# A hybrid decoder block on one core: logits in four column groups, new orders in the routing loop and at its end

## The chip, the cores and the metric

The kernel runs on one core of one Trainium2 chip. The metric is the device time of one execution in microseconds (us). Before the change the median of three runs was 2406.98 us (2404.17 to 2409.48).

## The reference, cut to what matters

1024 tokens of width 1024 go through a mixer (gated linear attention and a short convolution, merged by gates), then through a mixture of 32 experts of which each token uses four. The change touches only what lies between the two.

```python
x = x + jnp.matmul(mixed, w_out[l])
h = rms_norm(x, g_ffn[l])
logits = jnp.matmul(xt, w_router) + b_router      # (1024, 32), float32
top_logit, top_idx = lax.top_k(logits, TOP_K)     # 4 of 32
gates = jax.nn.softmax(top_logit, axis=-1)
...                                               # tokens sorted by expert
gu = lax.ragged_dot(xs, w_gate_up, group_sizes) + b_gate_up[e_sorted]
act = (lin + 1.0) * (gate * jax.nn.sigmoid(SWIGLU_ALPHA * gate))
out = lax.ragged_dot(act, w_down, group_sizes) + b_down[e_sorted]
y = jnp.einsum("tkd,tk->td", out_pairs, gates.astype(out.dtype))
```

## The kernel before

The program is a row of blocks, one after the other; each has a hand-written instruction stream for every engine, ordered by semaphores, and a block ends for all engines together, when the last of them is through. Five engines matter: PE (matmul), ACT, DVE (vector), POOL, which also issues the indirect DMAs, and SP, which issues the plain ones.

**The block `output_and_route`** multiplies the mixer's result with `w_out`, adds it to x, and routes. TT = 8 tiles of P = 128 tokens. The last panel of `w_out` (256 columns) is done tile by tile, in a loop in which the routing of the tiles in front is woven in. In iteration i PE does: two of the eight row blocks of the product of tile i; `turn(i-1)`, eight transposes of x2; three more row blocks; `rank(i-2)`; `logit(i-1)`, eight float32 matmuls whose left operand is `wr`, 128 x 32, and whose right one is a 128 x 128 block of the turned tile; the last three row blocks; `turn_back(i-1)`, a transpose of the 32 x 128 logits. ACT does per tile: `square` (sum of squares), `move` (the turned tile out of PSUM), `exps` of the tile in front (the exponentials of the four top logits), `root` (square root) and `move_low` (the logits out of PSUM). Exp and square root lie in different activation tables. DVE does per tile, in this order: `seats(i-2)` (the seat of each token in its expert's list, then the gates, written with them in `slots` and `place`, then the signal `slotted`), `select(i-2)` (two comparisons into `sel`, from which the rows of expert 0 are listed), `invert(i-1)`, `add(END-1, i)`, which signals `taken`, `choose(i-1)` (top 4) and `norm(i-1)` (the normed rows `ht`, stored to `h_rows` by SP). POOL writes, for each tile with `slotted`, TOP_K = 4 indirect scatters of `slots` into the table `slot_rows` (L1716); just ahead of the second scatter of tile 7 it waits for `first_listed` and for all stores of `h_rows` and issues the gather `xg` of the rows of expert 0 (L1713). SP stores x2 and ht of each tile and, between the x2 and the ht of the last tile, loads the weight panels m = 2, 3 of expert 0 (2 x 1 MB).

After the loop: `list_first` on DVE (L1841, L1843) gives the rows of expert 0; DVE splits a weight panel (L1906); then a chain of small operations (L1911 to L1939) with three matmuls plans the loop over the experts; DVE copies the plan (L1942 to L1947). PE transposes the gathered rows (L2049), ACT and DVE split them into `x_hi` and `x_lo` (L1774, L1951), and the block ends.

**The block `experts`** follows. SP loads m = 4 to 7 at once, and m = 8 to 11 when PE has done two panels. POOL issues the gather `xs_g` (L2331), waits for both gathers, reads the list of the next rows out of `slot_rows` (L2261, L2264) and then gathers the rows of the next 128-token unit (L2271). PE does panels 0 and 1, waits for `xs_g`, transposes it (L2686), does panels 2, 3, the small spill products (L2748), which run in four column groups of 32, then enters a loop over the units; in its first turn it transposes the next rows (L2679), and waits for them there. ACT and DVE split each panel (L2396, L2521); the first one on DVE in this block is L2656.

## Time and profile before

| | us |
|---|---|
| median of three runs | 2406.98 |
| lowest, highest | 2404.17, 2409.48 |
| the profiled execution | 2403.14 |
| its span, first to last instruction | 2401.6 |
| PE busy in the span | 2341.9 (98%) |
| DVE, ACT, POOL busy | 1629.0, 1273.5, 374.7 |

Times in rows are us from the span's start. A busy time of PE is not PE at its peak: matmuls overlap in the records. A timeline row gives start, duration, engine, line, operation, what it writes and reads, and in brackets the idle time ahead of it and what ended that. "POOLq" and "SPq" are the queues' own instructions. PEclk is the granted TensorE clock as a share of 2.4 GHz. The routing block runs its last tile loop from 999 to 1047, the experts start at 1072.

### The profile page before, as it was taken

The numbers are of one execution on the slowest core, as the hardware profiler recorded it, in microseconds if no ns is written. First come the engines' busy times: TensorE is split into PE (matmuls) and PEld (weight loads), VectorE is DVE, ScalarE is ACT, GpSimd is POOL, SyncE is SP. The second block draws the span as 40 slices with busy tenths as digits, with TensorE's granted clock in tenths as the row PEclk, the third lists the DMA queues.
The fourth block names the chain that finished last, engine by engine and source line by source line (L and its number), as shares of the span: only waits on it lengthen the run. The fifth ranks groups of instructions, "written<-read, shape, count | busy, mean of one in ns | idle before, by whom it ended". The sixth has DMA issues, their size and how long they took to land.

```text
span 2401.6 us, 40275 instructions
## 1 busy us (share of the span) xinstructions
PE 2341.9 (98%) x13219; PEld 1875.2 (78%) x13316; DVE 1629.0 (68%) x1669; ACT 1273.5 (53%) x1358; POOL 374.7 (16%) x412
## 2 busy tenths in 40 slices
PE   9999999999999999979999999999999999999996
PEld 7887778888888887957788777777777887777775
DVE  5213557766765353377798786878777987778877
ACT  6314663223233121365677666767656775667766
POOL 0000000000000002452211212112212122112110
PEclk9999999999999999989999999999999999999998
DMA  5233325454335235358999889989889997989998
GB/s 131 41 48 53 101 63 126 67 73 72 71 71 210 98 130 159 137 184 309 348 385 380 305 297 315 377 310 377 297 281 343 385 380 266 348 308 377 339 346 309
DMA packets 264860, 553.35 MB, mean 230 GB/s; under 512 B 29497, under 2 KB 76345, under 8 KB 263666
## 3 DMA queue, kind: packets, MB, share of 16 engines
q1 hardware_dynamic: 241490, 497.32, 61.9%
q0 software_dynamic: 23296, 55.03, 8.1%
q8 instruction: 48, 0.79, 0.1%
q14 instruction: 26, 0.21, 0.0%
HBM read 501.28 MB, written 51.02 MB: 230 GB/s over the span
## 4 chain that ended last, share of the span: by engine, by line
PE 53%; DMA 1%; issue 1%; DVE 0%; POOLq 0%; ACT 0%; DVEq 0%; ACTq 0%
PE m_y L2709 5%; PE m_y L2711 5%; PE m_y L2710 5%; PE m_gate L2711 5%; PE m_gate L2709 5%; PE m_lin L2711 5%; PE m_lin L2709 5%; PE m_gate L2710 5%; PE m_lin L2710 5%; PE m_spill L2748 4%; PE m_spill L2760 2%; PE m_turn L2693 1%; PE m_lin L2717 1%; PE m_gate L2679 1%; PE m_lin L2679 1%
## 5 line engine op out<-in xcount | busy, mean ns | idle before, releaser
L2521 DVE TENSOR_TENSOR m_w_lo<-raw,m_w_hi 128x2048 fp32r<-128x2048 f32 x382 | 868.7, 2288 | 245.2 <-ACT m_w_hi L2396 243.1
L2396 ACT CAST m_w_hi<-raw 128x2048 fp32r<-128x2048 f32 x382 | 730.9, 1914 | 353.3 <-PE m_lin L2711 243.9
L126 PE MATMUL c_bank<-h_hi_r,ring_hi 128*128 128x512 f32 x656 | 259.0, 395 | 1.9 <-DVE qk_r L1436 0.9
L2709 PE MATMUL m_gate<-m_w_hi,x_hi 128*128 128x512 f32 x508 | 215.8, 425 | 0.0
L2709 PE MATMUL m_y<-m_w_hi,m_a_hi 128*128 128x512 f32 x512 | 210.3, 411 | 1.8 <-DVE m_a_lo L2569 1.8
L2711 PE MATMUL m_y<-m_w_hi,m_a_lo 128*128 128x512 f32 x512 | 200.0, 391 | 0.0
L2710 PE MATMUL m_y<-m_w_lo,m_a_hi 128*128 128x512 f32 x512 | 199.7, 390 | 0.0
L2711 PE MATMUL m_gate<-m_w_hi,x_lo 128*128 128x512 f32 x508 | 198.8, 391 | 0.0
L2709 PE MATMUL m_lin<-m_w_hi,x_hi 128*128 128x512 f32 x508 | 198.4, 391 | 0.0
L2711 PE MATMUL m_lin<-m_w_hi,x_lo 128*128 128x512 f32 x508 | 198.3, 390 | 0.0
L2710 PE MATMUL m_gate<-m_w_lo,x_hi 128*128 128x512 f32 x508 | 198.2, 390 | 0.0
L2710 PE MATMUL m_lin<-m_w_lo,x_hi 128*128 128x512 f32 x508 | 197.8, 389 | 0.0
L128 PE MATMUL c_bank<-h_lo_r,ring_hi 128*128 128x512 f32 x480 | 187.3, 390 | 0.0
L905 ACT CAST ring_hi<-ring_raw 128x512 fp32r<-128x512 f32 x126 | 78.4, 624 | 189.7 <-PE c_bank L129 141.0
L126 PEld LDWEIGHTS c_bank<-h_hi_r,ring_hi 128*128 128x128 f32 x656 | 123.1, 188 | 34.7 <-issue 7.1
L2292 POOL DMA_INDIRECT y_rows<-m_y_out,m_slot_out x31 | 66.0, 2130 | 502.2 <-ACT m_y_out L2431 273.0
L129 PE MATMUL c_bank<-h_hi_r,ring_raw_r 128*128 128x512 f32 x368 | 143.6, 390 | 0.0
L172 ACT CAST ring_hi<-ring_raw 128x2048 fp32r<-128x2048 f32 x25 | 47.8, 1910 | 157.8 <-DMA ring_raw<-in_w_out 59.1
L176 DVE TENSOR_TENSOR ring_raw_r<-ring_raw,ring_hi 128x2048 fp32r<-128x2048 f32 x25 | 57.7, 2308 | 106.6 <-ACT ring_hi L172 106.5
L1055 DVE TENSOR_TENSOR ring_hi<-ring_raw,ring_hi 128x512 fp32r<-128x512 f32 x126 | 86.8, 689 | 59.6 <-ACT ring_hi L905 59.5
L2709 PEld LDWEIGHTS m_y<-m_w_hi,m_a_hi 128*128 128x128 f32 x512 | 96.6, 189 | 29.4 <-issue 6.9
L2271 POOL DMA_INDIRECT xg<-h_rows,slot_in x32 | 67.4, 2105 | 323.8 <-PE m_lin L2686 196.7
(425 smaller groups left out, 4606.0 us busy)
## 6 DMA issues: line engine op xcount, KB each, us to landing
raw<-in_w_gate_up SPq DMA_DIRECT2D x512, 512.0 KB, 11.3
raw<-in_w_down SPq DMA_DIRECT2D x256, 512.0 KB, 12.4
ring_raw<-in_w_in SPq DMA_DIRECT2D x31, 1024.0 KB, 9.6
gates<-work POOLq DMA_DIRECT2D x32, 256.0 KB, 4.4
work<-gates SPq DMA_DIRECT2D x8, 1024.0 KB, 7.2
v<-in_x SPq DMA_DIRECT2D x8, 512.0 KB, 5.3
r_rows<-work POOLq DMA_DIRECT2D x16, 256.0 KB, 3.0
o_rows<-v SPq DMA_DIRECT2D x8, 512.0 KB, 11.1
```

The lines of the kernel that those rows point to most:

```text
L126: pe.matmul(out, left_hi(k), right_hi(k), start=first and k == kts[0], stop=False, skip_group_check=True)
L128: pe.matmul(out, left_hi(k), right_lo(k), start=False, stop=False, skip_group_check=True)
L129: mm = pe.matmul(out, left_lo(k), right_hi(k), start=False, stop=last and k == kts[-1], skip_group_check=True)
L905: act.copy(ring.form(m)[0], ring.block(n, *((0, 0), (0, 0), (1, 0), (1, 0), (0, 1), (1, 1), (0, 1))[f])) \
L1055: dve.tensor_tensor(lo, (a11, a11, a21, a21, a12, a22, a12)[f], f32(hi), ALU.subtract) \
L2271: pool.indirect_dma_start(out=xg[:, :], out_offset=None, in_=h_rows[:, :], in_offset=bass.IndirectOffsetOnAxis(ap=slot_in[:, 0, 0:1], axis ...
L2396: act.copy(w_hi[:, p % WS].rearrange("p k b n -> p (k b n)"), raw[:, raw_slot(m)].rearrange("p k b n -> p (k b n)")).then_inc(signals.whi, 1)
L2521: dve.tensor_tensor(w_lo[:, p % WS].rearrange("p k b n -> p (k b n)"), raw[:, raw_slot(m)].rearrange("p k b n -> p (k b n)"), f32(w_hi[:, ...
L2709: pe.matmul(out, left_hi[:, kt], right_hi, start=False, stop=False, skip_group_check=True)
L2710: pe.matmul(out, left_hi[:, kt], right_lo, start=False, stop=False, skip_group_check=True)
L2711: mm = pe.matmul(out, left_lo[:, kt], right_hi, start=False, stop=kt == KT - 1, skip_group_check=True)
L2748: mm = pe.matmul(into(g), xs[:, 2 * (m % 4) + k], raw[:, raw_slot(m), k, :, P * g:P * g + P], start=False, stop=m % 4 == 3 and k == 1, ski ...
```

## The change

It does six things.

1. `logit`: the eight matmuls go to four column groups, k % 4, into the partitions 32g to 32g + 31 of `p_low`. `move_low` copies 128 partitions instead of 32, and `turn_back` is a float32 matmul with a constant `fold` (128 x 32, four identities), which adds the four parts.
2. ACT: `exps` are done for two tiles at a time, in odd iterations; in even ones `move_low` comes ahead of `root`.
3. DVE: `seats` no longer waits for the exponentials. The gates and the signal `slotted` are in a new `weigh`, called for tile i - 3 at the end of iteration i, and for tiles 5, 6, 7 after the planning chain (behind L1939). The two comparisons of `select` are one (`mark`) against a constant `seat_no`; at the end `norm(7)` comes ahead of `choose(7)`.
4. POOL: the tiles 0 to 4 are scattered (20 scatters), then it waits for `first_listed` and the stores and issues the gather `xg`; then tiles 5 and 6 (8 scatters), then the gather `xs_g`, all in the routing block. The four scatters of tile 7 are the first indirect DMAs of POOL in the block `experts`; ahead of the next list POOL waits until the last twelve scatters have landed (`end_sent`).
5. SP: the panels m = 2, 3 are loaded behind the last store of `h_rows`; m = 4 to 7 are loaded in the routing block too, when `xg` has landed.
6. The last block of DVE: `x_lo` is computed ahead of the copies of the plan.

```diff
@@ output_and_route: SP @@
-                if i == TT - 1:
-                    for m in range(2, 4):
-                        load_panel(sp, w_gate_up, w_down, raw, signals.raw_loaded, m, 0)
...
+            for m in range(2, 4):
+                load_panel(sp, w_gate_up, w_down, raw, signals.raw_loaded, m, 0)
+            sp.wait_ge(signals.gathered[0], 16)
+            for m in range(4, GU):
+                load_panel(sp, w_gate_up, w_down, raw, signals.raw_loaded, m, 0)
             sp.wait_ge(finished, 16 * (TT + 2))
-            sp.wait_ge(sent, 16 * TT * TOP_K)
+            sp.wait_ge(sent, 16 * (TT - LATE_T) * TOP_K)
@@ output_and_route: POOL @@
-            for i in range(TT):
+            for i in range(TT - LATE_T):
                 pool.wait_ge(slotted, i + 1)
                 for k in range(TOP_K):
-                    if i == TT - 1 and k == 1:
...
                     pool.indirect_dma_start(out=slot_rows[:, :],
...
+            pool.wait_ge(first_listed, 2)
+            for s in range(HT):
+                pool.wait_ge(stored[s], 16 * len(range(s, TT, HT)))
+            pool.indirect_dma_start(out=xg[:, :], out_offset=None, in_=h_rows[:, :],
...
+            for i in range(TT - LATE_T, TT - 1):
+                pool.wait_ge(slotted, i + 1)
+                for k in range(TOP_K):
+                    pool.indirect_dma_start(out=slot_rows[:, :],
...
+            pool.indirect_dma_start(out=xs_g[:, :], out_offset=None, in_=h_rows.rearrange("r (g c) -> (r g) c", g=NG),
...
@@ output_and_route: ACT @@
-            for i in range(TT - 1):
+            for i in range(TT):
                 square(i)
                 move(i)
-                if i >= 1:
+                if i % 2:
+                    root(i)
+                    move_low(i)
+                    if i >= 2:
+                        exps(i - 2)
                     exps(i - 1)
-                root(i)
-                move_low(i)
...
+                else:
+                    move_low(i)
+                    root(i)
             exps(TT - 1)
@@ output_and_route: DVE @@
+            def weigh(i):
                 dve.wait_ge(expd, i + 1)
                 step(dve.reciprocal(inv[:, i:i + 1], total[:, i:i + 1]))
...
             for i in range(TT):
                 if i >= 2:
                     seats(i - 2)
-                    select(i - 2)
+                    seat_key(i - 2)
+                    mark(i - 2)
...
+                if i >= 3:
+                    weigh(i - 3)
             seats(TT - 2)
-            select(TT - 2)
             invert(TT - 1)
+            seat_key(TT - 2)
+            norm(TT - 1)
             choose(TT - 1)
-            norm(TT - 1)
-            select(TT - 1)
+            mark(TT - 2)
+            seat_key(TT - 1)
+            mark(TT - 1)
             seats(TT - 1)
             list_first()
...
             dve.tensor_scalar(terms[:, 3 * W:4 * W], owner[:, :], expert[:, :], None, ALU.mult).then_inc(split_up, 1)
+            for i in range(TT - LATE_T, TT):
+                weigh(i)
@@ output_and_route: PE @@
                 for k in range(KT):
-                    mm = pe.matmul(p_low[0:E, 0:P], wr[:, k], xT[:, i % 2, k], start=(k == 0), stop=(k == KT - 1))
+                    g = k % NG
+                    mm = pe.matmul(p_low[E * g:E * (g + 1), 0:P], wr[:, k], xT[:, i % 2, k], start=k < NG,
+                                   stop=k >= KT - NG, skip_group_check=True)
...
-                pe.transpose(p_logits[:, 0:E], low[:, :], cst["ident"][0:E, 0:E]).then_inc(logged, 1)
+                pe.matmul(p_logits[:, 0:E], low[:, :], fold[:, :], start=True, stop=True,
+                          skip_group_check=True).then_inc(logged, 1)
@@ experts: SP and POOL @@
-            for m in range(4, GU):
-                load_panel(sp, w_gate_up, w_down, raw, signals.raw_loaded, m, 0)
...
-            pool.indirect_dma_start(out=xs_g[:, :], out_offset=None, in_=h_quarters,
...
             pool.wait_ge(signals.gathered[0], 16)
             pool.sem_inc(signals.rows_in, 1)
+            for k in range(TOP_K):
+                pool.indirect_dma_start(out=slot_rows[:, :],
...
             pool.wait_ge(signals.first_spill, 16)
+            pool.wait_ge(signals.end_sent, 16 * LATE_T * TOP_K)
```

## Rows read from the trace of the kernel before

**Rows 1.** The busy time of each engine in two stretches of 10 and 8 us

```profile
1057.00:1067.00 10.00, 1.36 (x3) 0.60 (x3) 6.28 (x26) 0.19 (x1) 6.30 (x6) 0.50 0.48 168
1072.00:1080.00 8.00, 8.00 (x25) 6.10 (x24) 6.21 (x3) 4.99 (x5) 1.87 (x1) 0.71 0.74 237
```

**Rows 2.** The timeline of DVE, one tile of the loop: start us, us, engine, line

```profile
1002.15 0.42 DVE L1793 TENSOR_TENSOR h_hi<-g_bank,h_hi 128x256 f32<-128x256 f32 x1 [2.55 <-PE g_bank L129]
...
1040.36 0.41 DVE L1793 TENSOR_TENSOR h_hi<-g_bank,h_hi 128x256 f32<-128x256 f32 x1
...
1045.23 0.16 DVE L1856 RECIPROCAL g_inv<-g_total 128x1 f32<-128x1 f32 x1 [0.89 <-ACT g_expo L1747]
...
1046.77 0.16 DVE L1798 RECIPROCAL g_stat<-g_stat 128x1 f32<-128x1 f32 x1 [0.45 <-ACT g_stat L1730]
1046.86 0.42 DVE L1793 TENSOR_TENSOR h_hi<-g_p_odd,h_hi 128x256 f32<-128x256 f32 x1
```

**Rows 3.** The timeline of PE, one logit and one spill product

```profile
1043.62 1.93 PE L1977 MATMUL g_p_low<-g_xT,g_wr 128*32 128x128 f32 x16
...
1087.70 3.63 PE L2748 MATMUL m_spill<-raw,m_xs 128*32 128x256 f32 x64
```

**Rows 4.** A group of instructions of ACT in the loop, busy, mean, idle ahead

```profile
L1730 ACT ACT_TABLE_LOAD x7 | 9.0, 1283 | 0.1
```

**Rows 5.** The timeline of DVE at the end of the routing and after

```profile
1051.40 0.16 DVE L1856 RECIPROCAL g_inv<-g_total 128x1 f32<-128x1 f32 x1 [0.60 <-ACT g_expo L1747]
...
1057.14 0.22 DVE L1841 TENSOR_SCALAR slot_in<-g_bank 128x1 int32<-128x1 f32 x1
...
1057.47 2.28 DVE L1906 TENSOR_TENSOR v_r<-raw,v_r 128x2048 fp32r<-128x2048 f32 x1
...
1062.35 0.23 DVE L1939 TENSOR_SCALAR g_terms<-g_owner,g_expert 33x60 f32<-33x60 f32 x1
...
1069.44 1.47 DVE L1951 TENSOR_TENSOR x_lo<-g_turned,x_hi 128x512 fp32r<-128x512 f32 x2 [4.55 <-ACT x_hi L1774]
...
1071.44 2.28 DVE L2656 TENSOR_TENSOR v_r<-raw,v_r 128x2048 fp32r<-128x2048 f32 x1
```

**Rows 6.** The timeline of POOL, last scatters, the two gathers

```profile
1057.98 2.60 POOL L1716 DMA_INDIRECT slot_rows<-g_slots,g_place  x1 [0.30 <-issue]
1063.06 0.99 POOL L1713 DMA_INDIRECT xg<-h_rows,slot_in  x1 [2.48 <-DMA h_rows<-g_ht]
...
1066.91 0.96 POOL L1716 DMA_INDIRECT slot_rows<-g_slots,g_place  x1 [0.30 <-issue]
1072.70 1.87 POOL L2331 DMA_INDIRECT xs_g<-h_rows,slot_in  x1 [4.83 <-issue]
```

**Rows 7.** The timeline of PE, the experts' start and its waits

```profile
1071.98 0.63 PE L2717 MATMUL m_lin<-b_split,m_pick 128*128 128x512 bf16 x1 [2.41 <-DVE m_pick L2527]
...
1081.36 0.43 PE L2686 MATMUL m_lin<-ident,xs_g 128*128 128x128 f32 x2 [1.27 <-DMA xs_g<-h_rows,slot_in]
...
1098.54 0.66 PE L2679 MATMUL m_gate<-ident,xg 128*128 128x128 f32 x4 [0.76 <-POOLq L2283]
```

**Rows 8.** The chain of work that ended last, between experts 0 and 1

```profile
1072.70 8.47 DMA xs_g<-h_rows,slot_in
...
1083.19 4.98 DMA slot_in<-slot_rows
...
1088.99 9.46 DMA xg<-h_rows,slot_in
```

**Rows 9.** The timeline of SP, the last stores and the panels 4 to 7

```profile
1050.37 5.57 SPq L1646 DMA_DIRECT2D h_rows<-g_ht  x2
...
1072.01 6.44 SPq L2876 DMA_DIRECT2D raw<-in_w_gate_up  x8
```

**Rows 10.** The waits of the DMA queue of SP: in total, times, longest

```profile
SPq L1648 <- DMA slot_rows<-g_slots,g_place: 13.1, 1, 13.1
```

**Rows 11.** The busy time at the very end of the run

```profile
2387.00:2388.00 1.00, 0.00 (x0) 0.00 (x0) 1.00 (x3) 1.00 (x3) 0.00 (x0) 0.72 1.03 418
```

More of the change, by code:

```diff
@@ L1556, in output_and_route @@
         wr = sb("wr", [P, KT, E])
[L1557 removed]
+        low, fold = sb("low", [P, P]), sb("fold", [P, E])
         br = sb("br", [P, E])
@@ L2108, in experts @@
 def experts(nc, w_gate_up, w_down, h_rows, y_rows, slot_rows, cst, now, where, expert_f, b_split, raw, w_first, x_hi,
-            x_lo, slot_in, xg, xs_g, signals, g_final, out):
+            x_lo, slot_in, xg, xs_g, end_slots, end_place, signals, g_final, out):
     h_quarters = h_rows.rearrange("r (g c) -> (r g) c", g=NG)
```

94 lines of the change are left out of this document (52 added, 42 removed).

## The prediction

> **What bounds the kernel now.** The page first: PE is busy for 98% of the span, and the chain that ended last runs through the experts' matmuls. A change that takes no matmul out of the experts can win only where PE waits. The busy times by stretch show where: between 1057 and 1067 PE is busy for 1.4 of 10 us at the half clock (0.50 is 1.2 GHz, 1.00 is 2.4 GHz), and the next stretch still starts at that clock [rows 1]. Ahead of it lies the loop over the eight tiles, in which PE looks full. The timelines of DVE, PE and ACT tell what a tile costs there; that of POOL and the chain of waits tell what follows. All times below are from one execution of 2403.14 us with a span of 2401.6; the median of three was 2406.98. I write T for the start of the last tile's add, 1046.86 [rows 2].
>
> **The loop, items 1 to 3.** From the first add at 1002.15 to T seven intervals take 44.7 us, a steady one 6.50 [rows 2]. PE: a logit is 16 records in 1.93 us, one after the other; the spill product shows 64 records twice as wide in 3.63 us, 57 ns each, since four column groups work at once [rows 3]. At that pace 16 records take 0.9 us at most, and at half of it, being half as wide, 0.45. I take 0.6, as the second row differs from the new logit in width alone: PE is free 1.3 us earlier per tile, at some 5.2 us. ACT: a tile has two table loads, one for the root and one for the exponentials, of 1283 ns [rows 4]; in pairs of tiles it has one each, which takes 1.28 us off an engine that was close behind PE. DVE: 6.50 less its two waits, 0.89 for an exponential and 0.45 for a root [rows 2], is 5.16 us of own work; two comparisons in one give back about 0.1, and the first wait goes, since `weigh` comes tiles later. So DVE, at 5.1, is late next, with PE just behind it. One wait comes back: in even tiles the root follows `move_low` and a table load of 1.28 us, while PE has only three eighths of a product left; I estimate 0.3 us in every other tile, 1.0 in all. The seven intervals take 7 x 5.1 + 1.0 = 36.7 us. **Minus 8.0.** Bounds: with the logit at 0.9, PE and its handovers set about 5.4, minus 6.5; with 0.45, minus 8.9. The wider copy in `move_low` costs nothing, since 128 partitions are as many elements per lane; the matmul with `fold` costs PE 0.1 more than the transpose did, within the 5.2.
>
> The Trainium skill (ScalarE: Activation LUTs, What ACT_TABLE_LOAD costs) gives about 2.66 us for each switch, load and drain together. The trace shows the load's 1.28 and only 0.1 us of idle time ahead of seven of them [rows 4], so that 1.28 stands. By the page's figure ACT would win 2.66 per tile, but the estimated 0.3 ahead of every other add would be 1.7, and the loop would win about 5 us less.
>
> **The end of the loop, items 2 and 3.** Old: `list_first` starts at 1057.14, T + 10.3 [rows 5]. New: DVE still does two norms and two choices in that stretch, now with `norm(7)` ahead of `choose(7)`, so the faster logit of tile 7 waits behind it. Off go the wait for an exponential, 0.60 [rows 5], one `weigh` of 0.4 and 0.2 of comparisons; the wait for the rank of tile 7, which the norm covered, comes back with 0.2. T + 9.3. The store of the last ht starts some 3 us sooner and without two panels in front of it, so that the 2.48 us that POOL waited for it [rows 6] goes. But DVE starts the split L1906, 2.28 us, right behind `list_first` [rows 5], and POOL's gather then falls into it. Such a split holds POOL: the scatter that began at 1057.98, within L1906 (1057.47 to 1059.75), took 2.60 us instead of 0.96 and ended 0.83 behind it; the gather of 1072.70 ended 0.85 behind L2656 [rows 5, 6]. So the gather is issued by about T + 12.7 instead of 1064.05. From there to the end of `x_lo` at 1070.91 it took 6.9 us [rows 5, 6], about half of it until it landed; DVE is at T + 19.6, and with an estimated 1.1 for the copies at T + 20.7. SP issues eight loads in 6.4 us [rows 9] from about T + 16.2 on: T + 22.6.
>
> **POOL at the block's end, item 4.** This is the term against the change. `slotted` of tiles 5 and 6 comes only behind L1939. From `list_first` to its end DVE needs 5.4 us as before (1057.14 to 1062.58) [rows 5]: T + 14.7, and 0.4 for the first `weigh`. POOL then issues eight scatters at 0.96 + 0.30 us [rows 6], 10.1 us, and the gather `xs_g`, 1.0: T + 26.2. A block ends with its last engine. That was DVE, with the end of `x_lo` at 1070.91, T + 24.05 [rows 5]; now it is POOL. **Plus 2.2.** Bounds: plus 1.5 if `weigh` is ready sooner, plus 3.2 if one or two scatters take the 1.6 us more that a DVE split can cost. Queued behind POOL is everyone, at the block's end; SP (T + 22.6), DVE and the early panels wait with it. So the panels m = 4 to 7, loaded some 10 us sooner, buy nothing: PE never waited for a panel there.
>
> **The experts' first unit, item 4 again.** PE started at 1071.98, waited 1.27 for `xs_g` and 0.76 for the next rows, and reached these at 1098.54, 26.56 behind its start [rows 7]. With `xs_g` issued before the block ends, the 1.27 goes. Without both waits PE would be there 24.5 behind its start. POOL's chain decides instead. Old: `xs_g` 8.47, some 2.0 of registers, the list 4.98, 0.8, the gather 9.46, landed at 1098.44 [rows 8], 27.4 behind the block's end. New: the first scatter of tile 7 starts where the gather `xs_g` did, 1.65 behind the block's end (1072.70) [rows 6], and falls into L2656, the next two into the splits L2521 of panels 2 and 3. Each ends about 0.85 behind the split that holds it, 2.3 us apart; the fourth finds DVE waiting for PE. The four end 10.1 behind the block's end (6.7 if nothing holds them). They have landed an estimated 2.0 later: SP waited for the old ones from 1055.94 on [rows 9] for 13.1 us [rows 10], 1.2 behind the last issue's end at 1067.87 [rows 6], and panels 8 to 11 load by now. Then 2.0 + 4.98 + 0.8 + 9.46 as before: 29.3. **Plus 1.9** against 27.4. Bounds: PE's own work ends the gain at minus 2.0 (scatters unheld, a gather of 6); plus 4.5 with slow landings and a held gather.
>
> The Trainium skill (SBUF — State Buffer, SBUF: two separate sides) says that the pair is an exclusive lock for a whole instruction, also against a DVE operation with two SBUF inputs. The trace agrees, with 2.60 against 0.96 us. By that rule `x_lo`, which has one input in PSUM, holds none of the eight scatters; held by it, they would end some 0.7 later, which lies within the bound of plus 3.2.
>
> **The sum.** -8.0 + 2.2 + 1.9 = -3.9. Behind the second unit PE runs on without a gap of note, so it stays. 2403.14 - 3.9 = 2399.2 for an execution like the profiled one; against the median, 2407.0 - 3.9 = 2403.1 us. About 0.2% (4.8 us) is what a measurement of this kernel can tell from no change.
>
> **The rivals.** A: the loop's gain arrives and little of it is lost. The four scatters slip between the splits or the gathers land faster than under the old load, so that PE reaches the second unit by its own work (minus 2.0 instead of plus 1.9), and the loop runs at DVE's pace. -8.0 + 2.2 - 2.0 = -7.8: 2399.2. For it: eight panel loads are out of the way by then. Against: the old gather met a full queue, and SP issues the next eight loads at the same place again.
>
> B: the clock falls. PE now waits 3.9 us for the second unit's rows. At the end of the run it had been idle for about 3 us when the clock went to the half [rows 11]; after the restart at 1071.98 the half clock lasted into the stretch 1072 to 1080, with 0.71 as its mean, which is 4.6 us at the half [rows 1]. That costs 2.3 us here: net -1.6, 2405.4.
>
> C: slower. The logit's groups do not overlap, because the eight matmuls share one bank and two of them each group. Then PE stays at 6.4 a tile, ACT's new order brings the root late, and the loop loses 0.7 instead of winning 8.0. The losses behind it stay: 0.7 + 2.2 + 1.9 = +4.8, with B's clock +7.1: 2411.8 to 2414.1. It decides from a logit of about 1.2 us on, where the loop's gain no longer pays for the 4.1 behind it. Against it: 64 spill records at 57 ns.
>
> D: the order on POOL does not hold, that is, tiles 5 and 6 are not late, because DVE reaches L1939 earlier than I say. Then SP ends the block, T + 22.6: another 3.6 off, -7.5, 2399.5. Against it: nothing in DVE's row of small steps gets shorter.
>
> **How the numbers follow.** My forecast has 0.50 (2403.1), B 0.20, A 0.18, D 0.05, C 0.07. Faster by over 0.2%: A, D and the lower fifth of the forecast's spread, 0.33. Slower: C, 0.07. The rest, 0.60, is within 0.2%. The range: below, the loop at minus 8.9 with A, about -9.5; above, the loop at minus 6.5 with plus 3.2 and the clock, about +2; a median of three moves by 2 us itself. 2397.0 to 2409.0; the forecast alone 2400.5 to 2405.5.
>
> **What would show it.** The adds of the loop 5.1 to 5.5 us apart, DVE without a wait for an exponential, the logit at 0.5 to 0.9. `list_first` some 9.3 behind T. POOL with a hole between the gather `xg` and the scatters of tile 5, then nine issues without a gap, and the other engines idle until they end. The experts' first matmul 5.8 us earlier than 1071.98; no wait for `xs_g`; scatters of tile 7 at over 2 us each; a wait of PE of about 4 us for the second unit's rows. I am wrong if the logit takes over 1 us, if PE waits less than 2 us or more than 6 at the second unit, or if the clock falls there.

## The result and the profile after

The changed kernel takes 2424.12 us (median of six runs, 2416.56 to 2425.43), against 2405.8 for the kernel before beside it: a ratio of 1.0068, 95% interval 1.0051 to 1.0084. It is **slower by 0.7%**, 16 us by the ratio and 18 by the medians. The forecast was 2403.1, and no change that can be measured. The profiled execution took 2425.38 us, with a span of 2423.8.

A second profile of the kernel before (run `c0_before`, below: 2407.09 us, span 2405.5) lies nearer to its median than the one that the prediction read. The table sets both beside the changed kernel, cut at the same points. T is the start of the last add.

| us | before, as in the prediction | before, second profile | forecast | after |
|---|---|---|---|---|
| first add of the loop | 1002.15 | 1004.75 | 1002.15 | 1004.11 |
| the seven intervals, to T | 44.71 | 47.54 | 36.7 | 48.06 |
| T to the experts' first matmul | 25.12 | 23.75 | 27.3 | 33.20 |
| from there to the second unit's rows | 26.56 | 26.21 | 28.5 | 32.91 |
| from there to the end of the span | 1303.1 | 1303.2 | 1303.1 | 1305.5 |

In the first profile PE's very first record of the experts (`m_gate`, 0.4 us ahead of `m_lin`) is missing, so its third row should read 24.7 and its fourth 27.0. Against the second profile, where nothing is missing there, the changed kernel's difference is -0.64 + 0.52 + 9.45 + 6.70 + 2.27 = 18.3 us, the whole difference of the two spans (2423.8 - 2405.5). So the question is threefold: where did the loop's 8 us go, why does the block end so late, and why does the second unit?

**The loop.** The timeline of DVE in the changed kernel, to set beside [rows 2, 5] (start us, us, engine, line):

```profile
1004.11 0.42 DVE L1812 TENSOR_TENSOR h_hi<-g_bank,h_hi 128x256 f32<-128x256 f32 x1 [2.55 <-PE g_bank L130]
1009.49 0.41 DVE L1812 TENSOR_TENSOR h_hi<-g_p_odd,h_hi 128x256 f32<-128x256 f32 x1
1014.10 0.42 DVE L1812 TENSOR_TENSOR h_hi<-g_bank,h_hi 128x256 f32<-128x256 f32 x1
...
1024.48 0.41 DVE L1812 TENSOR_TENSOR h_hi<-g_bank,h_hi 128x256 f32<-128x256 f32 x1
1030.71 0.41 DVE L1812 TENSOR_TENSOR h_hi<-g_p_odd,h_hi 128x256 f32<-128x256 f32 x1
1041.94 0.42 DVE L1812 TENSOR_TENSOR h_hi<-g_bank,h_hi 128x256 f32<-128x256 f32 x1 [1.71 <-DMA decay<-in_g_mix]
1052.17 0.42 DVE L1812 TENSOR_TENSOR h_hi<-g_p_odd,h_hi 128x256 f32<-128x256 f32 x1
...
1061.39 0.22 DVE L1862 TENSOR_SCALAR slot_in<-g_bank 128x1 int32<-128x1 f32 x1
1061.71 2.28 DVE L1939 TENSOR_TENSOR v_r<-raw,v_r 128x2048 fp32r<-128x2048 f32 x1
```

The first four intervals are the forecast's: 5.38, 4.61, 5.57, 4.81, mean 5.1. Then come 6.23, 11.23 and 10.23. `list_first` starts at T + 9.2. Here is what all engines do within the long interval:

```profile
1033.28 0.18 PE L2029 MATMUL g_bank<-g_chosen,before 128*128 128x32 bf16 x1
...
1034.27 0.64 PE L2013 MATMUL g_p_low<-g_xT,g_wr 128*32 128x128 f32 x16 [0.81 <-issue]
...
1037.42 0.28 PE L130 MATMUL g_bank<-ring_hi,h_lo_r 128*128 128x256 f32 x1 [0.42 <-issue]
1037.78 0.96 POOL L1720 DMA_INDIRECT slot_rows<-g_slots,g_place  x1 [0.30 <-issue]
1038.90 0.29 DVE L1871 TENSOR_TENSOR g_seated<-g_hot,g_bank 128x128 f32<-128x128 f32 x1 [4.54 <-remote]
1039.04 0.96 POOL L1720 DMA_INDIRECT slot_rows<-g_slots,g_place  x1 [0.30 <-issue]
...
1041.84 0.27 ACT L1762 COPY g_low<-g_p_low 128x128 f32<-128x128 f32 x1 [7.43 <-remote]
```

DVE waits for the rank (L2029), whose matmul is over in the records at 1033.46; its signal comes at 1038.88, 5.4 us late. ACT waits for the logit (L2013), over at 1034.92; its signal comes at 1041.82, 6.9 late. The add at 1041.94 waits for the product, over at 1037.70 (the profile names a DMA there that was long done); its signal comes at 1041.92. The nine matmuls of the product's last part lie behind the logit and are issued over 2.6 us, and yet the two signals come 0.1 us apart. "Remote" and "issue" say that the profile finds nobody to blame. The ends of matmuls are modelled, so a lag by itself may be the matmul's or its signal's; the 0.1 us speaks for signals that are held and let go together. They come 1.8 and 1.9 us behind the end of POOL's twelfth scatter without a break (1040.00). The Trainium skill (Perfetto Trace Analysis, Tensor Engine Instruction) says that the reported end of a matmul is an estimate, and that its semaphore is raised only when PSUM has acknowledged the writes. Here that signal comes 6.9 us behind the estimated end, and the trace can't tell whether the matmul or the signal took them.

**The block's end and the second unit.** POOL, SP and PE around 1067 to 1119, to set beside [rows 6, 7, 9]:

```profile
1058.40 18.35 SPq L2916 DMA_DIRECT2D raw<-in_w_gate_up  x12
...
1067.45 0.98 POOL L1732 DMA_INDIRECT slot_rows<-end_slots,end_place  x1 [2.60 <-DVE end_slots L1883]
...
1077.57 0.99 POOL L1735 DMA_INDIRECT xs_g<-h_rows,slot_in  x1 [0.30 <-issue]
1085.37 0.61 PE L2757 MATMUL m_gate<-b_split,m_pick 128*128 128x512 bf16 x1 [13.03 <-DVE m_pick L2567]
1086.59 1.76 POOL L2372 DMA_INDIRECT slot_rows<-end_slots,end_place  x1 [8.03 <-issue]
...
1118.28 1.12 PE L2719 MATMUL m_gate<-ident,xg 128*128 128x128 f32 x4 [9.09 <-POOLq L2321]
```

POOL's last issue ends at 1078.56, T + 26.4, where the forecast had it (T + 26.2). But the block ends at 1084.8. POOL's drain, its last instruction in the block, lasts until 1084.74; the last packets of its queue were moved at 1082.95. The busy time in three stretches (PE, PEld, DVE, ACT, POOL, PEclk, DMA share, GB/s) tells what stood in their way:

```profile
1072.00:1078.00 6.00, 0.34 (x2) 0.00 (x0) 2.33 (x8) 0.69 (x2) 4.48 (x6) 0.50 0.95 286
1079.00:1085.00 6.00, 0.00 (x0) 0.00 (x0) 0.00 (x0) 0.02 (x1) 0.00 (x0) 0.50 0.98 367
...
1119.00:1123.00 4.00, 4.00 (x14) 3.38 (x13) 0.00 (x0) 0.59 (x1) 0.57 (x1) 0.53 0.06 15
```

No engine works from 1079 to 1085, and the 16 DMA engines are full with the panels 4 to 7. The third stretch is the clock: PE waited 9.09 us, and when it started again it ran at 1.2 GHz for the next 4 us. The chain of waits in the experts' first unit (start, length, what), to set beside [rows 8]:

```profile
1093.93 6.15 DMA slot_rows<-end_slots,end_place
...
1102.15 5.25 DMA slot_in<-slot_rows
...
1108.22 9.97 DMA xg<-h_rows,slot_in
```

### The profile page after: what moved, and what is told of

Its sections match the earlier page's. It is cut to its first block, busy times and chain, and to the rows that moved or that the text cites. A ratio compares the mean times of both kernels' runs of the same rounds, so it can differ in the third digit from the quotient of the medians.

```text
span 2423.8 us, 40380 instructions
## 1 busy us (share of the span) xinstructions
PE 2348.1 (97%) x13323; PEld 1871.0 (77%) x13324; DVE 1628.3 (67%) x1664; ACT 1265.6 (52%) x1352; POOL 376.9 (16%) x417
## 4 chain that ended last, share of the span: by engine, by line
PE 53%; DMA 1%; issue 1%; DVE 0%; POOL 0%; POOLq 0%; ACT 0%; ACTq 0%; DVEq 0%
PE m_y L2749 5%; PE m_gate L2751 5%; PE m_gate L2749 5%; PE m_gate L2750 5%; PE m_lin L2749 5%; PE m_lin L2751 5%; PE m_lin L2750 5%; PE m_y L2751 5%; PE m_y L2750 5%; PE m_spill L2788 4%; PE m_spill L2800 2%; PE m_turn L2733 1%; PE m_gate L2757 1%; PE m_gate L2719 1%; PE m_lin L2719 1%
## 6 DMA issues: line engine op xcount, KB each, us to landing
ring_raw<-in_w_in SPq DMA_DIRECT2D x31, 1024.0 KB, 9.8
work<-gates SPq DMA_DIRECT2D x8, 1024.0 KB, 7.1
```

## The experiments

Fourteen runs. Those with a ratio were timed several times; the others are one execution each, made for their profile. The first four take the change apart.

### The groups alone

The kernel before, with the edits of item 1 only:

```diff
-                    mm = pe.matmul(p_low[0:E, 0:P], wr[:, k], xT[:, i % 2, k], start=(k == 0), stop=(k == KT - 1))
+                    mm = pe.matmul(p_low[E * g:E * (g + 1), 0:P], wr[:, k], xT[:, i % 2, k], start=k < NG,
+                                   stop=k >= KT - NG, skip_group_check=True)
...
-                act.copy(low[:, :], p_low[0:E, 0:P]).then_inc(low_moved, 1)
+                act.copy(low[:, :], p_low[:, 0:P]).then_inc(low_moved, 1)
...
-                pe.transpose(p_logits[:, 0:E], low[:, :], cst["ident"][0:E, 0:E]).then_inc(logged, 1)
+                pe.matmul(p_logits[:, 0:E], low[:, :], fold[:, :], start=True, stop=True,
```

> The kernel before, with only the logit in four column groups, the wide copy of it and the matmul with fold. The changed kernel lost its loop between the fifth add and the last (intervals 6.2, 11.2 and 10.2 us instead of 5.1). Theory 1, the groups are sound and the stall comes from the new orders: the loop here runs at ACT's pace, which still loads two tables per tile, intervals of about 5.7 us, logits of 0.65 us, no interval over 7, and the whole is 4 to 6 us shorter than before (about 2401). Theory 2, the groups bring the stall (PE's signals come late after them): intervals of 6 to 11 us at the sixth and seventh add here too, and the whole is 0 to 4 us longer than before. Theory 3, the stall was a chance of that execution: this run looks as in theory 1, and so do the loops of the other kernels of this set.

Measured: 2404.49 against 2405.14 us, ratio 0.9994 (0.9985 to 1.0004), no difference that can be measured. The intervals are 4.6, 6.3, 6.6, 7.1, 6.2, 7.1, 7.4. That is slower than theories 1 and 3 have it, and the last two lie at the lower edge of theory 2, which the next run rules out. What sets them, in its timeline:

```profile
1031.01 0.65 PE L1980 MATMUL g_p_low<-g_xT,g_wr 128*32 128x128 f32 x16
...
1032.58 1.28 ACT L1730 ACT_TABLE_LOAD   x1
...
1034.08 0.24 ACT L1743 COPY g_low<-g_p_low 128x128 f32<-128x128 f32 x1
...
1034.38 0.30 PEld L1986 LDWEIGHTS g_p_low<-g_fold,g_low 128*128 128x128 f32 x2 [1.67 <-ACT g_low L1743]
```

The logit takes 0.65 us instead of 1.93 [rows 3]. It is over at 1031.66, but ACT fetches it at 1034.08, behind two table loads, and PE's weight load waits 1.67 us: what the groups free on PE, PE waits for ACT. Signals of the rank came up to 2.0 us late here too, which they don't in the profile that the prediction read.

### Without the groups

The changed kernel, with the logit and the transpose of before: the diff above, the other way round.

> The changed kernel with the logit of before (sixteen matmuls one after the other, 1.9 us, and the transpose), all else new. By the prediction's own steps PE sets the loop here at 6.4 us a tile or more, the root comes late, and the loop is 0 to 2 us longer than before; everything behind it stays as in the changed kernel. Theory 1 (the new orders bring the stall): intervals of over 8 us late in the loop, the whole 20 to 30 us longer than before. Theory 2 (the groups bring it): no interval over 7.5 us, the whole 14 to 18 us longer than before, no worse than the changed kernel. Theory 3 (chance): the same as theory 2.

Measured: 2425.11, ratio 1.0077 (1.0060 to 1.0094). The loop takes 50.3 us, with intervals of 10.2, 7.4 and 7.3 at its end. Theory 2 falls: the groups do not bring the stall. The signals of a product and of the `turn_back` behind it came at 1039.33 and 1039.36, while their matmuls were over at 1035.4 and 1037.0.

### The gather xs_g behind the block

```diff
-            pool.indirect_dma_start(out=xs_g[:, :], ...)   # last of POOL in the block
+            pool.indirect_dma_start(out=xs_g[:, :], ...)   # first of POOL in experts
```

> The changed kernel, with the gather xs_g issued first thing behind the block instead of last thing in it. In the changed kernel the block's end came 6.2 us behind the end of that gather's issue (T + 32.6 against T + 26.4). Theory 1: the block ends only when POOL's outstanding indirect DMAs have landed, and a gather of 128 rows of quarters takes some 6 us, a small scatter 1 to 2. Then the block ends at about T + 27 here (the last scatter's issue ends at T + 25.4), PE starts the experts there, some 5.5 us earlier, PE gets a wait for xs_g of 1 to 4 us, and the whole is 2 to 6 us shorter than the changed kernel. Theory 2: the 6.2 us are something else (a stall of the whole block's end, code loading, ends that only look late), and the block ends 6 to 7 us behind POOL's last issue here too, T + 32, with the whole as in the changed kernel or 1 to 2 us longer. The loop: in both by whether the stall recurs in this execution.

Measured: 2423.40, ratio 1.0071 (1.0054 to 1.0088). POOL's last issue ends at T + 25.1, its drain at T + 31.5. Theory 1 in this form falls, since without the gather there are still 6.4 us. But the drain ends 1.7 us behind the last packet of POOL's queue (1082.20 and 1083.90), as in the changed kernel (1.8) and in the kernel before (1068.66 and 1070.63, 2.0): a scatter lands late as well when panels are ahead of it. The run after the next tests these panels.

The loop is the changed kernel's to 0.1 us in each interval (11.24 and 10.28): the stall is no chance.

### Item 4 undone

```diff
-            for i in range(TT - LATE_T, TT - 1):            # block: xg, tiles 5 and 6, xs_g
+            for i in range(TT - LATE_T, TT):                # tiles 5 to 7, xg behind the first of tile 7
...
             seats(TT - 2)
+            weigh(TT - 3)
+            weigh(TT - 2)
...
             seats(TT - 1)
+            weigh(TT - 1)
             list_first()
```

The gather `xs_g` and the `x_lo` splits go back to their old places as well.

> The changed kernel with item 4 undone: POOL issues all scatters in the block, xg behind the first one of tile 7, xs_g in the experts' program, and the x_lo splits stand behind the planning; weigh of tiles 5 and 6 stands ahead of the last invert, that of tile 7 ahead of list_first. The loop, the groups and SP's order stay new. Theory 1 (the loss at the block's end and at the second unit, 8.1 + 6.4 + 2.4 us, comes from item 4): list_first at T + 10.5, the block ends at about T + 24 by DVE, PE meets the second unit's rows 26.5 us behind its start with 1 to 2 us of waits; the whole is 12 to 17 us shorter than the changed kernel, so between 6 us shorter than before (no stall in the loop) and 4 longer (with it). Theory 2 (the loss comes from SP's order, panels 4 to 7 in the block): the block ends later than T + 28 or the waits of PE stay over 5 us, and the whole is still over 10 us longer than before.

Measured: 2414.43, ratio 1.0029 (1.0017 to 1.0042), 9.7 us shorter than the changed kernel. The second unit's rows come 25.2 us behind the experts' start, with 0.8 of a wait, as theory 1 has it; the 6.4 us there are the price of the four moved scatters. But the block ends at T + 33.4: POOL, which begins its first scatter at 1024.0 instead of 1014.2 since `weigh` comes late, has 12 left at T + 9, `xg` stands behind nine of these, and SP's panels 4 to 7 behind `xg` (24.45 us of issues from 1060.34 on). POOL's drain is over at T + 30.2 and SP's issues at T + 32.8, so here SP ends the block. Theory 1 holds for the second unit, theory 2 for the block's end.

### Panels 4 to 7 out of the block

```diff
-            sp.wait_ge(signals.gathered[0], 16)            # block: SP
-            for m in range(4, GU):
-                load_panel(sp, ..., m, 0)
+            for m in range(4, GU):                          # experts: SP, first
+                load_panel(sp, ..., m, 0)
```

> The changed kernel, with the panels m = 4 to 7 loaded behind the block again, at the place where the kernel before had them; panels 2 and 3, POOL's order and all else stay new. In the changed kernel POOL's drain at the block's end lasts until 1084.74, 6.2 us behind its last issue (1078.56), the last packets of its queue moved at 1082.95, and the panels' packets filled the 16 engines from 1072 to 1085; without xs_g in the block it was the same (drain to 1083.90, last packets at 1082.20, panels to 1084.1). Theory 1: the block ends only when POOL's transfers have landed, some 2 us behind their last packet, and these wait behind the panels. Without the panels a scatter lands 1 to 1.5 us behind its issue and the block ends at T + 29.5 to 30.5 instead of T + 32.6; the whole is about 3 us shorter than the changed kernel, less what the second unit loses as its scatters now meet these panels (0 to 3 us). Theory 2: POOL's drain takes its 6 to 7 us whatever the panels do: T + 32.6, the whole the same or 0 to 3 us longer.

Measured: 2417.69, ratio 1.0048 (1.0031 to 1.0064), 6 us shorter than the changed kernel. The timeline, and the busy time in one stretch (columns as above):

```profile
1074.10 0.98 POOL L1732 DMA_INDIRECT xs_g<-h_rows,slot_in  x1 [0.30 <-issue]
...
1078.89 0.61 PE L2756 MATMUL m_gate<-b_split,m_pick 128*128 128x512 bf16 x1 [10.18 <-DVE m_pick L2566]
```

```profile
1072.00:1078.00 6.00, 0.00 (x0) 0.00 (x0) 0.00 (x0) 0.00 (x0) 2.47 (x3) 0.50 0.08 24
```

The last packet moves at 1076.66, 1.6 behind the issue's end instead of 4.4; the drain ends at 1078.27 and PE starts at T + 30.2 instead of T + 33.2. **Theory 1 holds: the block ends with POOL's drain, that ends 1.6 to 2.0 us behind the last packet, and the packets wait behind the panels.** Its profiled execution (2416.61) is 8.8 us shorter than the changed kernel's: 1.8 by the first add, 1.6 in the loop (the same program with the same stall), 3.0 at the block's end and 3.0 in the second unit (29.9 instead of 32.9), less 0.7 behind it. The second unit does not lose by the move; it wins, which the expectation had the wrong way round.

### SP's new order alone, on the kernel before

```diff
-                if i == TT - 1:
-                    for m in range(2, 4):
-                        load_panel(sp, ..., m, 0)
+            for m in range(2, 4):                           # behind the last store of ht
+                load_panel(sp, ..., m, 0)
+            sp.wait_ge(signals.gathered[0], 16)
+            for m in range(4, GU):
+                load_panel(sp, ..., m, 0)
```

> The kernel before, with SP's new order alone: panels 2 and 3 behind the last store of ht, panels 4 to 7 in the block behind the gather xg. Theory 1, SP's issues and POOL's drain set the block's end: xg lands at about T + 20.5, SP issues eight loads in 6.4 us and ends at T + 27, POOL's last scatters land behind their packets; the block ends at T + 27 to 29 instead of T + 25, PE is no sooner at the second unit, and the whole is 2 to 4 us longer than before. Theory 2, the early panels harm only in the new order of POOL: the block's end stays within 1 us of T + 25 and the whole within 1.5 us of before.

Measured: 2409.51 against 2406.45, ratio 1.0014 (1.0004 to 1.0023), 3 us longer: theory 1. The queue of SP, and PE at the experts' start:

```profile
1073.28 5.52 SPq L2876 DMA_DIRECT2D raw<-in_w_gate_up  x8
```

```profile
1080.24 0.63 PE L2717 MATMUL m_lin<-b_split,m_pick 128*128 128x512 bf16 x1 [4.96 <-DVE m_pick L2527]
```

SP issues until 1078.8, and PE starts at T + 27.3 (its first record is missing here too). POOL's drain was over at 1075.19, so it is SP that ends the block here.

### The kernel before once more

> The kernel before, unchanged, to have a second profile of it beside these: the first add of the loop came at 1002.15 in its profile, and at 1003.5 to 1004.3 in those of the changed kernel and its four variants, all of which have 3.4 us at the half clock near 48 us, which the profile of before lacks. Theory 1, that is chance: this profile may show it too. Theory 2, it belongs to the program: this profile shows 1002.1 and no half clock there. The seven intervals are 6.5 us in any case.

Measured: 2407.09. The first add comes at 1004.75 and the half clock near 48 us is there: theory 1, chance. The loop, however, is not 6.5 us a tile "in any case". It takes 47.54 us, with intervals up to 8.07. DVE's waits for the rank:

```profile
1028.68 0.29 DVE L1850 TENSOR_TENSOR g_seated<-g_hot,g_bank 128x128 f32<-128x128 f32 x1 [1.75 <-remote]
...
1043.42 0.29 DVE L1850 TENSOR_TENSOR g_seated<-g_hot,g_bank 128x128 f32<-128x128 f32 x1 [1.48 <-remote]
...
1050.58 0.29 DVE L1850 TENSOR_TENSOR g_seated<-g_hot,g_bank 128x128 f32<-128x128 f32 x1 [1.59 <-remote]
```

The rank's signal comes 0.7 to 1.9 us late in five of eight tiles. In the profile that the prediction read, none did, although there too POOL issued the first eight scatters without a break:

```profile
1014.19 1.11 POOL L1716 DMA_INDIRECT slot_rows<-g_slots,g_place  x1 [31.10 <-DVE g_place L1860]
...
1024.01 1.16 POOL L1716 DMA_INDIRECT slot_rows<-g_slots,g_place  x1 [0.30 <-issue]
1026.53 0.96 POOL L1716 DMA_INDIRECT slot_rows<-g_slots,g_place  x1 [1.36 <-DVE g_place L1860]
```

The effect was there before the change, small and not in every execution.

### Scatters held back behind the loop

```diff
+            pool.wait_ge(slotted, TT - LATE_T)
             for i in range(TT - LATE_T):
-                pool.wait_ge(slotted, i + 1)
```

> The changed kernel, with the scatters of tiles 0 to 4 held until tile 4 is weighed, so that POOL issues nothing while the eight tiles' loop runs. Only the loop is of interest; the block's end comes some 10 us later by it. In the changed kernel the sixth and seventh intervals took 11.2 and 10.2 us, in which TensorE's signals came 5.4 and 6.9 us behind the modelled ends of its matmuls (rank 1033.46, logit 1034.92), while POOL issued 12 scatters without a gap from 1024.3 to 1040.0. Theory 1, POOL's unbroken scatters hold TensorE or its signals: without them all seven intervals take 4.6 to 5.6 us, the loop 36 to 38 us. Theory 2, it is the new orders of ACT and DVE, or something of TensorE's own: an interval of over 8 us at the sixth place here too, the loop 46 to 49 us.

Measured: the loop takes 36.02 us. All signals of rank and logit come within 0.05 us. DVE's adds:

```profile
1002.45 0.42 DVE L1812 TENSOR_TENSOR h_hi<-g_bank,h_hi 128x256 f32<-128x256 f32 x1 [2.55 <-PE g_bank L130]
...
1028.21 0.41 DVE L1812 TENSOR_TENSOR h_hi<-g_p_odd,h_hi 128x256 f32<-128x256 f32 x1
1033.02 0.41 DVE L1812 TENSOR_TENSOR h_hi<-g_bank,h_hi 128x256 f32<-128x256 f32 x1
1038.47 0.41 DVE L1812 TENSOR_TENSOR h_hi<-g_p_odd,h_hi 128x256 f32<-128x256 f32 x1
```

Theory 1. The whole is 2424.12, no better: PE's start falls from T + 33.2 to T + 51.5, since the scatters are now behind T.

### Half of the stores behind the loop

```diff
             for i in range(TT):
-                sp.wait_ge(taken, LAST + i + 1)
-                sp.dma_start(y_rows[i * P:(i + 1) * P, :], x2[:, i]).then_inc(finished, 16)
...
+            for i in range(TT):                             # behind the last store of ht
+                sp.dma_start(y_rows[i * P:(i + 1) * P, :], x2[:, i]).then_inc(finished, 16)
```

> The changed kernel, with the eight stores of y_rows moved behind the loop, so that half of the loop's store traffic is gone. Theory 1, the stores hold TensorE (it lost time at 1035 to 1038, when a store of 1 MB filled the 16 engines): the loop takes 36 to 38 us. Theory 2, POOL's scatters or the orders do it: the loop stays at 46 to 49 us, with the long interval at the sixth place. In both cases the block's end comes later, since eight stores of 0.5 MB stand ahead of the panels.

Measured: loop 48.04 us, the long intervals 11.23 and 10.23 to the hundredth. Theory 2: these stores have no part in it. Those of `ht` stayed in the loop, here and in every other run. The execution took 2421.15 us.

### Never more than four without a break

```diff
             for i in range(TT - LATE_T):
                 pool.wait_ge(slotted, i + 1)
+                if i:
+                    pool.wait_ge(sent, 16 * TOP_K * i)
```

> The changed kernel, with one wait more on POOL: before a tile's four scatters it waits until those of the tiles before have landed, so that it never issues more than four without a break. With all of them held back the loop took 36.02 us, with all of them in it 48.06, and the late signals of TensorE came while POOL issued its fifth to twelfth scatter without a break. Theory 1, only a long unbroken run of issues holds TensorE's signals: four at a time do as in the kernel before, a signal is at most 2 us late, and the seven intervals take 37 to 41 us. Theory 2, each scatter costs by itself: some 16 of them still fall into the loop and it takes 44 to 48 us. In both cases POOL falls back and the block's end comes 3 to 8 us later behind the last add.

Measured: 38.70 us, one signal 2.05 us late, no other over 1. Theory 1. POOL's drain at the block's end is 9.3 us further behind T than in the changed kernel (T + 41.9, T + 32.6), more than expected, and the whole is 2422.04.

### The first scatter ten us later

```diff
-                pool.wait_ge(slotted, i + 1)
+                pool.wait_ge(slotted, max(i + 1, 3))
```

> The changed kernel, with POOL's first scatter held until tile 2 is weighed (about 10 us later than in the changed kernel), so that twelve then stand ready at once. Theory 1, the late signals follow POOL's unbroken run: the first five intervals and the sixth up to some 4 us into the run are as without scatters (4.6 to 5.6 us each), a signal comes over 2 us late only from about the fifth scatter of the run on, so at the seventh interval or behind the loop, and the loop takes 36 to 43 us. Theory 2, the place in TensorE's program or the tile number decides: the sixth interval takes over 10 us here too, the loop 46 to 49.

Measured: 37.55 us; the first six intervals are those without scatters (4.61 to 5.57), the seventh 7.00. The run of scatters starts at 1032.3, and the signals of matmuls that end at 1035.4 to 1036 come 0.6 and 1.6 us late, at 1042 2.1, at 1045 5.2 and at 1054 7.6. POOL's first scatter, and ACT's fetch of the logit that was over at 1044.89:

```profile
1032.34 1.21 POOL L1720 DMA_INDIRECT slot_rows<-g_slots,g_place  x1 [49.02 <-DVE g_slots L1883]
...
1050.07 0.27 ACT L1762 COPY g_low<-g_p_low 128x128 f32<-128x128 f32 x1 [6.12 <-remote]
```

Theory 1: the lag follows the run of scatters and grows with it, wherever the program stands. The execution took 2423.20 us.

### What remains of the change, on the order of before

```diff
-                if i >= 3:
-                    weigh(i - 3)
+                if i >= 2:
+                    weigh(i - 2)
...
-                if i % 2:
-                    root(i)
...
+                root(i)
+                move_low(i)
+                if i:
+                    exps(i - 1)
```

With it, items 4 to 6 are undone; the diff is against the changed kernel.

> What the runs so far would keep of the change, on the order of the kernel before: the logit in four groups, one comparison for two, weigh behind norm one tile later than before (so that POOL's first scatters start some 3 us later, not 10), ACT's order root, move_low, exponentials in every tile; POOL's block with all 32 scatters, xs_g in the experts' program, the x_lo splits behind the planning, and SP's panels where the kernel before had them. Theory 1, the parts are understood: ACT has 5.7 us of own work a tile and sets the loop at 5.9 to 6.2 us, late signals of up to 2 us fall on some tiles, the seven intervals take 41 to 45 us (in three profiles with the order of before they took 44.7, 47.5 and 49.0), the block ends at T + 24 to 26, the second unit's rows come 25 to 27 us behind the experts' start, and the whole is 1 to 4 us shorter than before. Theory 2, POOL's scatters (5.04 us of issue in a tile of 6) leave so few breaks that TensorE's signals come over 2 us late as in the changed kernel: an interval of over 9 us, and the whole as before or 1 to 6 us longer.

Measured: 2411.09 against 2405.99, ratio 1.0018 (1.0009 to 1.0027). The timeline around the stall:

```profile
1016.61 0.41 DVE L1803 TENSOR_TENSOR h_hi<-g_p_odd,h_hi 128x256 f32<-128x256 f32 x1
...
1021.91 0.42 DVE L1803 TENSOR_TENSOR h_hi<-g_bank,h_hi 128x256 f32<-128x256 f32 x1 [0.20 <-PE g_bank L130]
...
1031.44 0.95 POOL L1718 DMA_INDIRECT slot_rows<-g_slots,g_place  x1 [0.30 <-issue]
...
1033.96 0.27 ACT L1758 COPY g_low<-g_p_low 128x128 f32<-128x128 f32 x1 [5.98 <-remote]
...
1034.07 0.42 DVE L1803 TENSOR_TENSOR h_hi<-g_p_odd,h_hi 128x256 f32<-128x256 f32 x1 [4.42 <-DMA decay<-in_g_mix]
```

Theory 2. Four intervals of 4.6 to 5.3 us, the fastest of all runs; but a tile has 5.04 us of scatters, POOL issues twelve from 1016.4 on without a break, and the next two intervals take 12.2 and 9.5. The loop's 47.22 us are no more than the 47.54 of the kernel before in its second profile, though. The loss lies behind it: POOL issues twelve more without a break until 1063.67, and the rank of tile 7, over at 1060.10, signals at 1065.62, 5.5 us late. The gates of that tile and POOL's last scatters wait for it, and PE starts at T + 29.8 instead of T + 23.75:

```profile
1067.52 3.07 POOL L1731 DMA_INDIRECT slot_rows<-end_slots,end_place  x1 [3.85 <-DVE end_slots L1874]
...
1079.20 0.61 PE L2749 MATMUL m_gate<-b_split,m_pick 128*128 128x512 bf16 x1 [2.01 <-DVE m_pick L2559]
```

No run was measurably faster than the kernel before.

### POOL busy without DMAs, and with plain ones

In both, tiles 0 to 4 are scattered behind the loop, and at each tile POOL does four fills of a buffer, or six plain loads.

```diff
+                for k in range(4):
+                    step(pool.memset(blank[:, :, :], 0))
```

```diff
+                for k in range(6):
+                    pool.dma_start(out=f32(blank[:, 6 * i + k, 0:8]), in_=w_router[0:P, 0:8]).then_inc(plain, 16)
```

> The changed kernel, with the scatters of tiles 0 to 4 held back behind the loop, and in their place, at each tile, four fills of a buffer by POOL (about 1.2 us each) that touch no DMA. Theory 1, it is POOL's issuing of DMAs that holds TensorE's signals: the loop takes 36 to 38 us, as with a quiet POOL (36.02). Theory 2, a POOL that is busy without a break is enough: a signal comes over 2 us late and the loop takes over 41 us. The block's end, some 20 us later than in the changed kernel, is of no interest.

> The same, with six plain loads by POOL at each tile in their place (128 x 32 bytes from the router's weights into a buffer that nobody reads; 0.5 us of issue each in this kernel). Theory 1a, every DMA that POOL issues holds the signals: late signals of over 2 us and a loop of over 40 us here too. Theory 1b, only the indirect ones do, with their list of places that POOL reads: the loop takes 36 to 38 us.

Measured: with fills 38.87 us, with plain loads 35.98; in neither is one signal of rank or logit more than 0.05 us late (the executions took 2435.98 and 2432.80 us). A tile of POOL in each:

```profile
1029.17 4.87 POOL L1720 MEMSET g_blank<- 128x1280 int32 x4 [1.19 <-DVE g_slots L1886]
```

```profile
1028.47 3.19 POOL L1720 DMA_DIRECT2D g_blank<-in_w_router  x6 [1.14 <-DVE g_slots L1887]
```

Neither kept POOL without a break: it pauses 1.2 us between the fills of two tiles and 1.1 to 2.3 us between the loads. The fair comparison is with four scatters and a break, which came with a signal 2.05 us late above, and with 0.7 to 1.9 us in the second profile of the kernel before. At 4.87 us a tile, near the scatters' 5.04, the fills did nothing of the kind, so it isn't POOL's being busy at that share. The plain loads took only 3.2 us. So **only indirect DMAs did it** (theory 1b), but a run of twelve plain DMAs or fills without a break, as the scatters had it, was not made. The fills cost the loop 2.9 us in another way, which the expectation had missed. DVE beside a fill:

```profile
1031.66 1.18 DVE L1843 CAST g_index_f<-g_index 128x4 f32<-128x4 uint32 x1
```

This copy of four elements takes 0.17 us in the changed kernel. The Trainium skill (SBUF — State Buffer, SBUF: two separate sides) says that DVE and POOL share one pair of ports as an exclusive lock and that TensorE never waits on anyone at its own. The first half agrees, with 1.18 against 0.17 us. The second half speaks of SBUF's ports, not of signals: that the loop takes 48.06 us with scatters and 36.02 without does not refute it, and no run here shows by what way they delay TensorE.

## Why the prediction was wrong

Step by step, in the prediction's order.

- **The loop's own work: right.** The logit at 0.6 was 0.65, and the loop of 36.7 us was 36.02 with a quiet POOL. Two errors cancel in that, which is luck: DVE's own work is 4.8 us a tile and not 5.1 (the intervals of 4.81 have no wait), and its wait for the root in every other tile is 0.5 to 1.0 us and not 0.3. Groups overlap, so rival C had the wrong cause for its sign.
- **The loop, -8.0: wrong.** The failed step is the one that was not costed. "DVE, at 5.1, is late next, with PE just behind it" stops at the engines that wait for each other; POOL does not stand in that list. Its scatters, 4 x (0.96 + 0.30) = 5.04 us a tile [rows 6], left a break of 1.5 us in a tile of 6.5 (but for the first two tiles) and leave none in one of 5.1. From the third or fourth scatter of a run on, TensorE's signals came late, by up to 2.3 us within the first four, by up to 7.7 behind them. The first profile's eight scatters in a row without a late signal show that such a run need not do it each time; but all twelve other profiles with scatters in the loop have late signals, and the three without scatters there have none. `weigh`'s later place, costed at nothing, adds to it: POOL starts 20.2 us behind the first add instead of 12.0 and is behind from then on. The clock fell within the stall (0.52 in 1041 to 1048), which lengthened the seventh interval, together with the late signals of a logit (1.4 us) and a product (2.3).
- **`list_first` at T + 9.3, xg issued by T + 12.7, POOL's last issue at T + 26.2: right**, measured T + 9.2, T + 12.7, T + 26.4.
- **The block's end, +2.2: mis-sized by its rule.** "A block ends with its last engine" is right, but POOL's part was ended at its last issue. It ends with the drain, 2.8 us behind the last issue in the kernel before (1067.87, 1070.63), and there DVE hid it by 0.3 us only. The 4.83 us of "issue" ahead of POOL's first instruction of the next block [rows 6] held it. Then the panels, of which the prediction says that their earlier loading "buys nothing": it cost 3 us, as it put their packets ahead of the scatters'. In all 8.1 instead of 2.2, from T + 25.1 to T + 33.2 (8.5 with the missing record).
- **The second unit, +1.9: the mechanism right, a term mis-sized.** Four scatters, three of them held by DVE's splits (1.76, 2.77, 1.90, 0.96 us), end 10.1 us behind the block's end, as forecast. From the last issue's end to the landing it took 5.2 us (1094.89 to 1100.08), not 2.0: SP loads the next panels from 1093.0 on. The list and the gather are near the forecast, 5.25 and 9.97 against 4.98 and 9.46. +6.4 in all (6.0 with the missing record), above the bound of 4.5.
- **Rival B's mechanism came true, not its 2405.4:** PE waited 9.09 us, not 3.9, and the clock fell; the last row of the table, +2.4 us, is near the 2.3 that B gave it. These are two of the three signs that the prediction named for its being wrong.
- **The sum.** Against the profile that it read, the span is 22.2 us longer: 3.3 in the loop, 8.1, 6.4 and 2.4 behind it, and 2.0 by the first add, which is chance (it came at 1002.0 to 1004.75 in all kernels). The terms behind the loop alone would have given the sign: even with the loop's 8 us, 8.1 + 6.4 + 2.4 stand against it.

What is open: by what way indirect DMAs hold TensorE's signals, and whether it is the matmul or its signal that is late. The runs show when it happens and how long, not where. An indirect gather was not tried in place of the scatters, nor a scatter with fewer rows, nor plain DMAs or fills without a break. Why eight scatters in a row did nothing in one execution is not known either. And the loops of most variants rest on one profile each, though the changed kernel and three variants that keep its loop agree within 0.1 us (48.04 to 48.13); a fourth, without the panels in the block, took 46.44. The 3.4 us at the half clock near 48 us appeared in some executions and not in others, before and after.

## What to carry to other kernels

An engine off the path is still a rate: before shortening a loop, divide each helper's issue time per turn by the new length, and where that comes near one, ask what an unbroken run of it does to others. A block's end waits for POOL's transfers to land, so whatever is queued ahead of them on the DMA engines, weights loaded early above all, is paid for there. And one profile of the kernel before may be its luckiest: a second one would have shown late signals, and a loop 2.8 us longer.

## What the hardware showed that was not expected

- While POOL issued indirect scatters without a break, signals of TensorE reached DVE and ACT late in 12 of 13 profiles: up to 2.3 us for matmuls that ended within the first four scatters of a run, up to 7.7 for those within the next four, and up to 7.6 later. With plain DMAs (six a tile of 0.5 us) or fills (four of 1.2 us), each with a break of over 1 us a tile, none was over 0.05 us late.
- The held signal of the logit in the long stall came 1.8 us behind the end of POOL's twelfth scatter in the changed kernel (1040.00, 1041.82) and in three variants that keep its loop, 1.5 us in the mix. Other signals came in the midst of a run, as one with the later first scatter (1050.05).
- POOL's drain at a block's end ended 1.6 to 2.3 us behind the last packet of its queue in 15 of 16 profiles, and 3.0 in the one with plain loads.
- A scatter of 128 rows landed 1.1 to 1.2 us behind the end of its issue when the DMA engines were idle, and mostly 4 to 5.6 us behind it with panels in flight (5.2 in the changed kernel's second unit).
